# State rows with the normaliser in them, a lower rank for the LayerNorm apply, and the last Fourier column first, in an eight-core mLSTM and Fourier backbone step

## What is computed

```python
z = u @ w_in + b_in                       # q, k, v, o, gates, fourier, conv, merge gates
h, (C, n, m) = mlstm_bidir(q, k, v, ...)  # chunks of 128 tokens, two directions, 4 heads of 256
h_m = sigmoid(o) * norm(h) * mlstm_norm_g
h_f = fft2(fourier input).real            # per group of 256 channels
h_c = cb * conv3(cc * cx)
merged = sigmoid(gm)*(h_m @ w_br_mlstm) + sigmoid(gf)*(h_f @ w_br_fourier) + sigmoid(gc)*(h_c @ w_br_conv)
x = layer_norm(ALPHA*x + g1 * (merged @ w_out))          # first LayerNorm of the layer
x = layer_norm(ALPHA*x + g2 * ((silu(a)*b) @ w_down))    # a, b = split(modulate(x) @ w_gate_up)
```

## Time and profile before

| | us |
|---|---|
| median of 3 runs shown | 2181.45 |
| lowest and highest of them | 2177.61 and 2279.78 |
| the profiled execution | 2179.41 |
| its span on the slowest core (core 1), first to last instruction | 2178.4 |
| the shortest span among its cores (core 2) | 2158.0 |

### The profile page before, as it was taken

How to read it: one execution, slowest core, us unless ns; L and a number is a source line. 1 busy time by engine, 2 the same in 40 slices (tenths; PEclk the granted TensorE clock), 3 DMA queues, 4 the chain that set the end, 5 groups by cost and what they waited for, 6 DMA issues and landing times.

```text
span 2178.4 us, 29412 instructions; the slowest of 8 cores (2158.0 to 2178.4 us)
## 1 busy us (share of the span) xinstructions
PE 2081.5 (96%) x11756; PEld 1072.8 (49%) x11756; DVE 1124.2 (52%) x2123; ACT 822.2 (38%) x1387; POOL 680.7 (31%) x1087
## 2 busy tenths in 40 slices
PE   2998999999999999999999999999999999999997
PEld 1555664444444444444446666544444443444446
DVE  2767764555444862222586777455544478222256
ACT  1566642222222561111355665422222247111125
POOL 2466651123211530101454766311122145000022
PEclk9999999999999999999999999999999999999999
DMA  9766446675334345543136754533433326422212
GB/s 199 168 136 130 101 129 114 110 155 102 70 62 109 81 71 97 100 94 73 46 91 146 145 131 107 113 49 58 117 58 68 54 78 112 70 47 39 54 39 78
DMA packets 120857, 206.98 MB, mean 95 GB/s; under 512 B 53882, under 2 KB 81544, under 8 KB 119056
## 3 DMA queue, kind: packets, MB, share of 16 engines
q0 software_dynamic: 35552, 124.90, 33.4%
q1 hardware_dynamic: 85168, 80.19, 12.4%
HBM read 272.67 MB, written 39.94 MB: 144 GB/s over the span
## 4 chain that ended last, share of the span: by engine, by line
PE 83%; DVE 7%; DMA 5%; POOL 3%; ACT 2%; issue 1%; DVEq 0%; SPq 0%
PE ps L195 83%; DMA kW<-wpack 2%; DVE x_77 L237 1%; DVE x_76 L237 1%; DMA wst_192<-wpack 1%; DVE x_78 L237 1%; ACT x_78 L225 0%; DMA oC<-C_275 0%; DMA oC<-C_130 0%; DMA C_273<-C0n 0%; DMA oW_166<-wpack 0%; DMA oC<-C_129 0%; DMA cpk<-cpk 0%; DVE x_77 L249 0%; DMA hm_79<-hn_271 0%
## 5 line engine op out<-in xcount | busy, mean ns | idle before, releaser
L249 DVE SCALAR_TENSOR_TENSOR x_76<-ps,g1a,x_76 128x512 f32<-128x512 f32 x32 | 24.0, 749 | 63.6 <-PE ps L195 63.4
L225 ACT ACTIVATE sg_333<-ps,cpk 128x512 f32<-128x512 f32 x26 | 17.8, 686 | 52.8 <-PE ps L195 50.1
L225 ACT ACTIVATE sa_234<-ps 128x512 f32<-128x512 f32 x22 | 13.1, 596 | 65.2 <-PE ps L195 65.2
L249 DVE SCALAR_TENSOR_TENSOR x_77<-ps,g1a,x_77 128x512 f32<-128x512 f32 x32 | 23.7, 746 | 27.0 <-PE ps L195 26.5
L225 ACT ACTIVATE sg_187<-ps,cpk 128x512 f32<-128x512 f32 x26 | 17.8, 686 | 50.4 <-PE ps L195 47.7
L225 ACT ACTIVATE mo_200<-ps,cpk 128x512 f32<-128x512 f32 x21 | 14.4, 687 | 57.7 <-PE ps L195 57.7
L195 PE MATMUL ps<-u_73,kW 128*128 128x512 bf16 x128 | 32.4, 403 | 3.0 <-DMA kW<-wpack 2.8
L225 ACT ACTIVATE sa_382<-ps 128x512 f32<-128x512 f32 x22 | 13.1, 596 | 58.3 <-PE ps L195 58.3
L225 ACT ACTIVATE mo_346<-ps,cpk 128x512 f32<-128x512 f32 x21 | 14.4, 687 | 54.6 <-PE ps L195 54.6
L249 DVE SCALAR_TENSOR_TENSOR x_78<-ps,g1a,x_78 128x512 f32<-128x512 f32 (+1 forms) x40 | 24.9, 635 | 19.6 <-PE ps L195 19.6
L225 ACT ACTIVATE sa_236<-ps 128x512 f32<-128x512 f32 x22 | 13.1, 596 | 57.5 <-PE ps L195 57.5
(11 more groups left out here) (1991 smaller groups left out, 5763.2 us busy)
## 6 DMA issues: line engine op xcount, KB each, us to landing
x_76<-xin SPq DMA_DIRECT2D x2, 2048.0 KB, 16.0
kW<-wpack POOLq DMA_DIRECT2D x8, 512.0 KB, 6.9
qW<-wpack POOLq DMA_DIRECT2D x8, 512.0 KB, 7.7
xspill<-x_77 SPq DMA_DIRECT2D x2, 2048.0 KB, 10.5
wst_192<-wpack SPq DMA_DIRECT2D x8, 512.0 KB, 4.1
r_167<-wpack POOLq DMA_DIRECT2D x8, 512.0 KB, 6.8
r_169<-wpack POOLq DMA_DIRECT2D x8, 512.0 KB, 6.4
r_170<-wpack POOLq DMA_DIRECT2D x8, 512.0 KB, 5.9
```

The lines of the kernel that those rows point to most:

```text
L225: ins = A.activation(out=rap(out), in_=rap(in_), func=func, **kw)
L249: ins = V.scalar_tensor_tensor(out=rap(out), in0=rap(a), scalar=rap(s), in1=rap(b), op0=op0, op1=op1)
```

## The change

Four things:

- A state leaves with its normaliser: one row of 514 numbers (2056 bytes) per partition, in one DMA. The copies on POOL into `nall`, the tile and the DMA `on_raw` are gone; the host splits the columns.
- `APPLY` gives the operations of `ln_apply` of the first LayerNorm a bias: 100 for block 1, 130 for block 2 (block 0 and the second LayerNorm: 0). A number that is higher ranks behind, so gate products of the FFN rank ahead of them. The affine steps on ScalarE keep 300.
- `mirrored(7)` stands ahead of the three blocks of column 7, instead of at the gate `gf` of block 0.
- In `settle`, each transfer's duration for the next planning is the longest of the four replays, not that of the plain one.

```diff
-            mean = (t + sum(self.replay(s)[0] for s in range(3))) / 4
+            runs = [self.replay(s) for s in range(3)]
+            mean = (t + sum(r[0] for r in runs)) / 4
...
-            self.took = took
+            self.took = {k: max([v] + [r[1][k] for r in runs]) for k, v in took.items()}
...
+APPLY = ((0, 100, 130), (0, 0, 0))
...
-    oC_d = dout("oC", [6, DEPTH, 2, H, DH, DH])
-    on_d = dout("on_raw", [DEPTH, 128, 96])
+    oC_d = dout("oC", [6, DEPTH, 2, H, 128, 514])
...
-    nall = const("nall", [128, 2, 48])
...
     def ln_apply(l, which, b, rs, nm, lo, n, gp):
+        R.bias = base = APPLY[which][b]
...
                 R.bias = LATE[which]
             R.act(z, z, AF.Identity, scale=colp[:, l, cg + j:cg + j + 1], bias=colp[:, l, cb + j:cb + j + 1])
-            R.bias = 0
+            R.bias = base
...
+        R.bias = 0
...
-                    R.dma("sp", oC_d[seg, l, d, h].rearrange("(k p) e -> p k e", p=128), Cn[:, :, 0:256], "o" + Cn[:].tensor.name)
-                    i = seg * 8 + d * 4 + h
-                    R.copy(nall[:, :, i:i + 1], Cn[:, :, 256:257], eng="pool", n=2, cost=208)
+                    R.dma("sp", oC_d[seg, l, d, h], Cn[:].rearrange("p a n -> p (a n)"), "o" + Cn[:].tensor.name)
...
-        R.dma("sp", on_d[l], nall[:].rearrange("p a b -> p (a b)"), "on")
...
+            if j == 7:
+                mirrored(j, wf)
             for b in range(3):
...
-                    if b == 0 and name == "gf":
+                    if b == 0 and name == "gf" and j < 7:
                         mirrored(j, wf)
```

More of the change, by code:

```diff
@@ L829, in build_program @@
     R = Rec(nc)
-    R.outputs = {t.tensor.name for t in (y_d, oC_d, on_d, om_d)}
+    R.outputs = {t.tensor.name for t in (y_d, oC_d, om_d)}
     R.act_window = 400
@@ L1931 @@
         r = res.results[core]
-        y, oC = r["y"].reshape(3, 128, 8, 512).transpose(0, 3, 2, 1).reshape(NTOK, D), r["oC"]
-        on, om = r["on_raw"].reshape(DEPTH, 128, 2, 48), r["om_raw"].reshape(DEPTH, 2, 4, 12)
+        y, oC = r["y"].reshape(3, 128, 8, 512).transpose(0, 3, 2, 1).reshape(NTOK, D), r["oC"].reshape(6, DEPTH, 2, H, 128, 2, 257)
+        om = r["om_raw"].reshape(DEPTH, 2, 4, 12)
         pa, pb_ = prompts_of[core]
@@ L1945 @@
         for s, p in segs:
-            nC[p] = oC[s]
-            blk = on[:, :, :, s * 8:(s + 1) * 8].reshape(DEPTH, 128, 2, 2, H)
-            nn[p] = blk.transpose(0, 3, 4, 2, 1).reshape(DEPTH, 2, H, DH)
+            C = oC[s].transpose(0, 1, 2, 4, 3, 5).reshape(DEPTH, 2, H, DH, 257)
+            nC[p], nn[p] = C[..., 0:256], C[..., 256]
             nm[p, :, 0, :] = om[:, 0, :, opos(0, 2 * s + 1)]
```

## The result

The changed kernel takes 2214.05 us (median of 4 runs, 2204.81 to 2354.2) against 2180.54 before: 1.4% slower, ratio 1.0144 with a 95% interval of 1.0099 to 1.0189. The forecast was 2158 with a range of 2144 to 2182. Ratios here, and the medians given for the experiments, leave out executions in which one die ran at a lower clock than the other; counted so, the changed kernel's median is 2211.9.

A forecast was written before the change was run, and what follows sets the result against it. TensorE, busy 2081.5 of 2179 us, was taken as the bound. Gates -5.8, last column -2.8, merge start -4, heads -9 and two zeros gave -21.6: 2179.4 to 2157.8, so 2158, range 2144 to 2182.

The forecast's parts named there:

- What bounds the kernel: Whole kernel: TensorE is the bound, busy 2081.5 of 2179 us; only its idle 97.5 us and lower-clock stretches can be won.
- The row: State writes with normaliser in one row: 96 POOL copies, 17.6 us, go; 0 on the path, bounds 0 and -1.
- a write may also land 0.5, 1.0 and 0.8 us later than now: State writes: bounds on slower landing, from cached-state loads with 2056-byte rows landing in 2.6, 3.6 and 9.5 us.
- rival 3: Heads: longer rows hold state buffers longer; eleven writes with under 9 us of cover cost 36 us, 2194; chance 0.06.
- The estimate of about 5.3 us for 8 pieces under traffic: State writes: if 16 pieces wait their turn at 0.40 us each, 8 land in about 5.3 instead of 8.56.
- The heads, -9 and 0: Heads: longer covers end layer 0's buffer and oW stalls, -9 (bounds -18, +10); layer 1 0 (bounds -8, +8).
- The merge's start, -4: Layer 0's merge start: wf multiplies behind the sums end TensorE's wait for ac_190; gain 4, bounds 0 and 4.8.
- The last column, -2.8: Last Fourier column first: TensorE's wait for mg_0 goes, 1.4 in each layer, 2.8; bounds 0 and 2.9.
- Gate products, -5.8: First LayerNorms: gate products ahead of the apply shorten TensorE's g_0 waits; 2.9 a layer, 5.8 both, bounds 0 and 13.0.
- two groups in hand that need no new bank: Layer 0's first LayerNorm: from 773.8 these and one more group occupy TensorE until 779.0, then a new 2.6 us wait.
- The sum: Whole kernel: all terms together -21.6 us, from 2179.4 to 2157.8, so 2158, a gain of 1.0%.

## Why the prediction was wrong

**What bounds the kernel**: right. TensorE's idle time in the span went from 96.9 (2178.4 less 2081.5) to 121.2 us (2215.1 less 2093.9), and its busy time went up by 12.4 for the same matmuls at the lower mean clock (0.986 for 0.992): 24.3 and 12.4 are the 36.7 of the spans.

**The row: here it failed**, and with it the terms of the heads, -9 and 0 with upper bounds of +10 and +8, where +11.4 and +27.4 were measured. It failed in two steps. The first was the bound: "a write may also land 0.5, 1.0 and 0.8 us later than now", taken from loads with rows of 2056 bytes. Measured were 0.7, 3.9 and 8.2. A load of such rows reads them, and says nothing of what a write does where two rows meet. With room between the rows the bound would have held for the median (0.1 later); the longest is 2.4 later, but so it is in this order with the old rows (11.0). The second was rival 3, which named the right wait and the right place. It put the slowness down to the rows' length, which costs nothing (2048 bytes end to end: 2167.3), and had it too cheap and too unlikely: 9.5 us for eleven writes, 2194, a chance of 0.06. Against that stand a median of 6.5 and a longest of 16.9. The estimate of about 5.3 us for 8 pieces under traffic is wrong as well: the longest landing is 10.2 with 8 pieces of 2048 bytes and 11.0 with 16 of 1024, in the same order.

The Trainium skill, "DMA: Bandwidth & Descriptors", section "Queues, rings and completion order", has an engine change queues only at the end of a packet of typically 9 to 17 descriptors. The landings of 8 and of 16 pieces, 10.2 and 11.0, are in line with that; no run shows the packets themselves. The Trainium skill, the same page, section "How a descriptor splits into AXI transactions", has a descriptor's first transaction start at the 256-byte boundary below its start. An estimate worked out from that is nine transactions for a row of 2056 bytes at every start that is a multiple of 8, and it agrees with the runs on rows that have room (2166.6 in one run 8 bytes off, 2168.7 on the boundary). It also gives nine for the rows end to end, so this rule does not tell the slow rows from the fast.

**The heads, -9 and 0**: measured between the chain's places with room for the rows (461.96 for the wst load, 1122.42 for the end of layer 0 and 1792.18 for the LayerNorm's sum in layer 1), layer 0's heads gain 6.8 us and layer 1's heads and merge 0.8, though mg_0 alone was to give 1.4 there. The sizes came near, but by luck, as the reason was wrong: with settle's old line this place is at 459.85 and with the row alone at 462.76 (6.0 us earlier than before), so the covers that I counted in the new order are not what won it. A wait that I had not named stands there too, wp, 3.3 us.

**The merge's start, -4**: wrong, the stage is +1.0. The wf multiplies stand behind the sums as I said, and the wait for ac went, but nb and mo need the same weights, which land no sooner (18.71 us in the chain before, 19.55 after). A stall by a load moved to the next user of that load.

**The last column, -2.8**: the waits went and came back with the edit; the time does not show it.

**Gate products, -5.8**: the first g_0 runs 2.83 us earlier against the LayerNorm's sum (785.36 less 761.52, before 775.87 less 749.20): 2.8 as worked out, and the new wait behind rn_1 came in layer 1 (1.56 us). But the step "two groups in hand that need no new bank" looked at the banks and not at the weights. The new order takes the third pair's first group as the next one, and its load was not there (4.97 us in layer 0, 1.11 in layer 1): layer 0 +1.0, layer 1 -4.0, in all -3.0 instead of -5.8. With the loads in the other order the same two stages are 4.1 and 4.4 us shorter than before (740.30 to 1115.01 and 1783.46 to 2135.88 in that kernel's chain), 8.5 with what the clock gives back.

**The sum**, 21.6, became about 10 with room for the rows (2178.7 less 2168.7). Of these, 5.9 come with the row alone, which the prediction had put at 0 on the path, and 4.3 with the three other edits.

## What to carry to other kernels

Where rows go to HBM side by side, give each row room of its own: with 2304 bytes for 2056 the same program is 0.6% faster than before instead of 1.4% slower, and a multiple of 32 (2080) did nearly as well in one run (2170.4). Price a changed write by writes, not by loads of the same shape. When a wait is taken away, look for what the same instructions wait for next, buffers, weights and their place in the load queue alike; a reordering that shows no gain may have one once a load is moved.

## What the runs showed of the hardware

Rows of 2056 bytes end to end, where three seams of four lie inside a piece of 32 bytes, written in one DMA, made the median landing 6.5 us instead of 2.7 with room between them, with nothing else changed. Rows that begin 8 bytes and end 16 bytes past a multiple of 256, alone in their pieces, stay near the usual (3.4, one run), and so do seams inside a 64-byte line (3.1, one run). I had not expected the first, nor that the second costs next to nothing. How the hardware handles the shared piece, no run shows.
